# The norms of a delta-rule recurrence: quadrant products or wide products on TensorE

## What is computed

```python
kk = heads(k * k_k)
kk = kk / jnp.maximum(jnp.sqrt(jnp.sum(kk * kk, axis=-1, keepdims=True)), 1e-12)
...
S = S * w_t + sa * (kk_t * a_t) + v_t * k_t
y_t = S @ r_t
...
var = jnp.mean(jnp.square(y - mean), axis=-1, keepdims=True)
y = (y - mean) * lax.rsqrt(var + RWKV_GN_EPS) * ln_g + ln_b
```

## Time and profile before

| | |
|---|---|
| time, median of 3 runs | 871.68 us (871.65 to 872.04) |
| profiled execution, first to last instruction | 873.2 us |
| instructions in that span | 17369 |
| PE busy | 815.8 us, 93% |
| DVE busy | 460.3 us, 53% |
| ACT busy | 240.4 us, 28% |
| POOL busy | 278.8 us, 32% |

### The profile page before, as it was taken

One profiled execution on the slowest core, in us unless ns is written; L12 is line 12 of the kernel. 1 busy time (PEld: TensorE's weight loads), 2 busy tenths in 40 slices (PEclk: granted clock), 3 DMA queues, 4 the chain that ended last, 5 costly groups with the idle time before them and its releaser, 6 DMA issues. The chain is left out here.

```text
span 873.2 us, 17369 instructions
## 1 busy us (share of the span) xinstructions
PE 815.8 (93%) x7175; PEld 544.7 (62%) x7175; DVE 460.3 (53%) x1154; ACT 240.4 (28%) x581; POOL 278.8 (32%) x267
## 2 busy tenths in 40 slices
PE   8999999999999999799888999999999999999950
PEld 8557544544444355777777455555788888888830
DVE  3750478887830136467664244434645555454534
ACT  6220111112200143455543112221233223232214
POOL 5810000000499501452741100000135565543332
PEclk9999999999999999999999999999999999999995
DMA  9934433445111123000000881112889989888639
GB/s 315 324 90 135 145 120 121 139 158 172 37 38 36 27 70 133 18 3 4 4 4 20 308 325 48 49 73 96 325 296 301 303 285 273 277 267 261 206 73 367
DMA packets 79719, 136.35 MB, mean 156 GB/s; under 512 B 17213, under 2 KB 51226, under 8 KB 79642
## 3 DMA queue, kind: packets, MB, share of 16 engines
q1 hardware_dynamic: 69338, 118.44, 39.0%
q0 software_dynamic: 10304, 16.82, 8.2%
HBM read 124.18 MB, written 29.92 MB: 176 GB/s over the span
## 5 line engine op out<-in xcount | busy, mean ns | idle before, releaser
L792 PE MATMUL banks<-REG_W 128*128 128x512 f32 (+2 forms) x832 | 274.6, 499 | 0.9 <-DVE pend L1988 0.5
L792 PEld LDWEIGHTS banks<-REG_W 128*128 128x128 f32 (+1 forms) x832 | 125.9, 182 | 135.3 <-issue 133.8
L792 PE MATMUL banks<-REG_W,REG_Y 128*128 128x512 f32 x256 | 118.3, 599 | 1.4 <-DVE REG_Y L2236 1.1
L1434 ACT ACTIVATE REG_P<-banks 128x256 f32<-128x256 f32 (+2 forms) x126 | 53.5, 463 | 156.8 <-PE banks L792 137.7
L792 PE MATMUL banks<-REG_P 64*64 64x64 f32 (+3 forms) x2752 | 79.5, 230 | 13.1 <-issue 8.9
L792 PEld LDWEIGHTS banks<-REG_P 64*64 64x64 f32 (+1 forms) x2752 | 67.6, 135 | 23.0 <-issue 16.4
L1434 ACT ACTIVATE REG_Y<-banks,mod,s 128x128 f32<-128x128 f32 x136 | 51.2, 457 | 85.8 <-PE banks L1386 85.8
L792 PEld LDWEIGHTS banks<-REG_W,REG_Y 128*128 128x128 f32 x256 | 45.6, 191 | 44.3 <-issue 44.2
L792 PEld LDWEIGHTS banks<-REG_Y,REG_P 128*128 128x128 f32 (+1 forms) x616 | 63.1, 181 | 7.0 <-issue 7.0
L792 PE MATMUL banks<-REG_Y,REG_P 128*128 128x128 f32 (+1 forms) x616 | 66.6, 276 | 0.1
L636 POOL TENSOR_TENSOR REG_P<-REG_P 128x1040 f32<-128x1040 f32 x2 | 4.8, 2390 | 175.8 <-DVE REG_P L1801 175.8
(11 more groups left out here) (295 smaller groups left out, 1108.1 us busy)
## 6 DMA issues: line engine op xcount, KB each, us to landing
REG_P<-in_w_ada SPq DMA_DIRECT2D x20, 1024.0 KB, 6.2
REG_W<-in_w_in SPq DMA_DIRECT2D x17, 512.0 KB
REG_P<-in_moe_w_gate SPq DMA_DIRECT2D x17, 512.0 KB, 8.3
REG_W<-in_moe_w_gate SPq DMA_DIRECT2D x16, 512.0 KB, 6.4
REG_W<-in_moe_w_up SPq DMA_DIRECT2D x16, 512.0 KB, 10.7
REG_W<-in_moe_w_down SPq DMA_DIRECT2D x16, 512.0 KB, 16.7
REG_P<-in_moe_w_up SPq DMA_DIRECT2D x14, 512.0 KB, 14.9
REG_P<-in_moe_w_down SPq DMA_DIRECT2D x12, 512.0 KB, 21.2
```

The costliest lines, as they stand in the source:

```text
L792: return pe.matmul(o_, l, r, start=start, stop=stop, skip_group_check=True)
L1434: return act.activation(o_, i_, f, **kw)
```

## The change

The six norms inside the turns use the same wide functions as numbers 1 and 8. The sums become 4 products of 128x128 by 2 columns, the turn one transpose to 8 rows of 128, the spreading 4 products with 8 rows of weights and 128 columns. Inside the turns the results lie elsewhere than for the outer two: the sums in columns 256 to 263 of bank 4, the turned roots in bank 6, the spread ones in banks 6 and 7. The semaphores count one for each step in place of two.

```diff
+            def outer(k):
+                return k in (front_norm(0), tail_norm(TURNS - 1))
+
             def norm_sums(k, squares, count):
...
+                at = 0 if outer(k) else 256
                 for n in range(2):
                     for p in range(2):
-                        c = n * 4 + p * 2
+                        c = at + n * 4 + p * 2
                         last = mm(PS[4][:, c:c + 2], squares[:, p, n * P:(n + 1) * P], bones[:, 0:P:64])
                 last.then_inc(s["w_ss"], 1)
 
             def norm_flip(k):
                 pe.wait_ge(s["w_nrp"], k)
-                pe.transpose(PS[4][0:8, P:2 * P], nrp[:, 0:8], ident[:, :]).then_inc(s["w_nrt"], 1)
+                pe.transpose(PS[4 if outer(k) else 6][0:8, P:2 * P], nrp[:, 0:8], ident[:, :]).then_inc(s["w_nrt"], 1)
 
             def norm_back(k):
...
                 for p in range(2):
                     for n in range(2):
-                        last = mm(PS[5][:, p * W2 + n * P:p * W2 + (n + 1) * P], sel[0:8, n * 2 + p, :], nrT[0:8, :])
+                        at = p * W2 + (n * P if outer(k) else 0)
+                        last = mm(PS[5 if outer(k) else 6 + n][:, at:at + P], sel[0:8, n * 2 + p, :], nrT[0:8, :])
                 last.then_inc(s["w_nrb"], 1)
-
-            corners = ((0, 0), (1, 1), (1, 0), (0, 1))
-
-            def turn_sums(k, squares, count):
...
-                        for h, c in corners:
-                            last = mm(PS[4 + h][cr(c), at:at + 1], squares[hb(h), p, n * P + CH * c:n * P + CH * c + CH],
-                                      ones[hb(h), 0:1])
...
-            def turn_flip(k):
-                pe.wait_ge(s["w_nrp"], k)
-                for c, g in corners:
-                    last = mm(PS[6 + c][hb(g), P:P + CH], nrp[cr(c), :], identq[cr(c), :])
...
-            def turn_back(k):
...
-                for p in range(2):
-                    for n, h in corners:
-                        last = mm(PS[6 + n][hb(h), p * W2:p * W2 + P], sel[cr(n), n * 2 + p, 64 * h:64 * h + 64], nrT[cr(n), :])
...
                         if tail:
-                            turn_sums(tail_norm(m - 1), sqt, tail_squares(m - 1))
+                            norm_sums(tail_norm(m - 1), sqt, tail_squares(m - 1))
...
-                dve.wait_ge(s["w_ss"], 2 * k - 1)
-                ts(nrm[:, :].rearrange("p (a h) -> p h a", h=2), banks[:, 4:6, 256:260], a, b, op0, op1).then_inc(s["w_nrm"], 1)
+                dve.wait_ge(s["w_ss"], k)
+                at = 0 if outer(k) else 256
+                ts(nrm[:, :], PS[4][:, at:at + 8], a, b, op0, op1).then_inc(s["w_nrm"], 1)
...
-                dve.tensor_copy(nrT[:, :].rearrange("p (c t) -> p c t", c=2), banks[:, 6:8, P:P + CH]).then_inc(s["w_nrT"], 1)
+                dve.wait_ge(s["w_nrt"], k)
+                dve.tensor_copy(nrT[0:8, :], PS[4 if outer(k) else 6][0:8, P:2 * P]).then_inc(s["w_nrT"], 1)
```

More of the change, by code:

```diff
@@ L1179, in turn @@
                         pe.wait_ge(s["w_tha"], min(m + 2, TURNS))
-                        turn_flip(tail_norm(m - 1))
+                        norm_flip(tail_norm(m - 1))
                     if tail and l == 4:
-                        turn_back(tail_norm(m - 1))
+                        norm_back(tail_norm(m - 1))
                     if more and l == 4:
-                        turn_sums(front_norm(m + 1), sq, front_squares(m + 1))
+                        norm_sums(front_norm(m + 1), sq, front_squares(m + 1))
                     for n in range(2):
@@ L1204, in turn @@
                         pe.wait_ge(s["w_nbu"], tail_norm(m - 1))
-                    turn_flip(front_norm(m + 1))
+                    norm_flip(front_norm(m + 1))
                 for p in range(2):
@@ L1222, in turn @@
                 if more:
-                    turn_back(front_norm(m + 1))
+                    norm_back(front_norm(m + 1))
                 for n in range(2):
@@ L1529, in squash @@
                     act.wait_ge(s["w_lora"], m)
-                    act.wait_ge(s["w_ss"], 2 * front_norm(m - 1) - 1)
+                    act.wait_ge(s["w_ss"], front_norm(m - 1))
                 z6 = pT[:, B_LORA, PAD + m * W2:PAD + (m + 1) * W2]
@@ L1931, in norm_turned @@
             def norm_turned(k):
[L1932 to L1936, removed]
-                dve.tensor_copy(nrT[:, :].rearrange("p (c t) -> p c t", c=2), banks[:, 6:8, P:P + CH]).then_inc(s["w_nrT"], 1)
+                dve.wait_ge(s["w_nrt"], k)
+                dve.tensor_copy(nrT[0:8, :], PS[4 if outer(k) else 6][0:8, P:2 * P]).then_inc(s["w_nrT"], 1)
             def back(k):
-                if k in (front_norm(0), tail_norm(TURNS - 1)):
-                    dve.wait_ge(s["w_nrb"], 1 if k == front_norm(0) else 2 * k - 2)
+                dve.wait_ge(s["w_nrb"], k)
+                if outer(k):
                     return PS[5].rearrange("p (a n t) -> p a n t", a=2, n=2)
-                dve.wait_ge(s["w_nrb"], 2 * k - 1)
                 return banks[:, 6:8, :].rearrange("p n (a x) -> p a n x", a=2)[:, :, :, 0:P]
```

13 lines of the change are left out of this document (removed).

## The result

The changed kernel takes **873.58 us** (median of 16 runs, 871.08 to 877.47), the kernel before, run beside it, 871.66 us (16 runs). The ratio is 1.0026, 95% interval 1.0015 to 1.0037: slower by 2.3 us, between 1.3 and 3.2. The forecast was 875.4 us in a range of 871.0 to 881.0, slower by 0.2 to 1%.

The account below looks back on a forecast made before the run. PE was taken as the bound, held at times by instruction packets about 3.85 us apart. Added PE time 12.3, less 2.9 hidden, less 5.7 from fewer packets, gave +3.7 us: 875.4 us, range 871.0 to 881.0.

Parts of the forecast that it names:

- What bounds the turns: In the recurrence's four turns, PE is the bound and at times stands until its next instruction packet arrives, 9.9 us.
- The 3.85 us of the prediction: In dense stretches of the turns, two instruction packets of PE in a row cannot start closer than about 3.85 us.
- Time on PE, +12.3 us: Wide sums, turn and spreading of six norms, at 0.11 us a load plus switches, lengthen PE's work by 12.3 us.
- I take 0.2 us each way: Around each wide set on PE, going from quadrants to the whole array and back costs 0.2 us each way.
- What is hidden, -2.9 us: In four places of the turns PE waits anyway for ACT or DVE, which covers 2.9 us of the added work.
- The other three covers: DVE waits after the tail's sums, 0.5 us, after the front's spreading, 1.1 us, and before turn 3, 0.7 us.
- What fewer packets give back, -5.7 us: 468 fewer PE records in the turns are 1.86 packets, 7.1 us; four fifths of it, 5.7 us, comes back.
- The walk through a turn: In turn 0 both later pauses go; in turns 1 to 3 boundaries partly only move, hence four fifths of 7.1.
- The four turns longer by about 4 us: Sign expected in the profile after: the recurrence's four turns last about 4 us longer, mostly the turns with two norms.
- The feed gives nothing back: Rival: in the turns packet boundaries only move and dense packets pause as before; +9.4 us, 881.1 us; chance 0.15.
- The feed decides, faster: Rival: wide work fits under 3.85 us a packet in the turns; -7.1 us, 864.6 us, or half, 868.1; chance 0.10.
- No difference: Rival: with array switches at half, 0.1 us each way, the change nets +0.1 us, 871.8 us, not measurable; chance 0.20.

Follow-up runs that it names:

- 64 columns: The change with the wide sums of the six inner norms moving 64 columns in place of 2, against the kernel before: 873.75 us, ratio 1.0013.
- change again: The changed kernel run once more, unaltered, against the kernel before: 874.86 us, ratio 1.0029.
- change, sums twice: The change with the wide sums of the six inner norms computed twice, against the kernel before: 882.62 us, ratio 1.0100.
- quadrant sums twice: The kernel before with the quadrant sums of the six norms computed twice, 384 records more, nothing wide: 877.87 us, ratio 1.0068.
- bfloat16 squares: The kernel before with squares and ones of the norms' sums in bfloat16, 192 records fewer inside the turns: 869.46 us, ratio 0.9970.
- the three parts: Wide forms put into the kernel before for the six inner norms: sums alone, ratio 1.0006; spreading alone, 1.0010; turn and spreading, 1.0007.

## Why the prediction was right, and where its sum was off

**What bounds the turns: right.** PE is the bound and packets of its program hold it. Both directions with nothing made wide moved the time as the step said, +5.9 us for 384 records more and -2.6 for 192 fewer, though the profile of the second shows no gain in the turns. The packets of the instruction queue are in the trace themselves: of the 29 distances from one start to the next in the four turns of the kernel before, 22 lie between 3.4 and 4.2 us, and in none of the twelve profiles is one under 3.28 us. The 3.85 us of the prediction are thus a middle value and not the least distance. The Trainium skill, "Runtime: NRT & Kernel Launch", section "Instruction fetch mechanics", lets the crossing from block to block be mostly hidden; in these dense stretches the runs disagree.

**Time on PE, +12.3 us: too high.** With the change and 64 columns the clock stayed at full, so it shows this term by itself. The four turns of the kernel before, then of that one:

```profile
340.30:478.10 137.80, 120.13 (x3821) 103.76 (x3821) 87.77 (x185) 69.41 (x185) 58.00 (x42) 1.00 0.08 27
```

```profile
338.70:476.00 137.30, 127.40 (x3587) 109.48 (x3586) 87.59 (x185) 69.37 (x185) 58.00 (x42) 1.00 0.08 27
```

PE is busy 7.3 us longer, in turns that are no longer: 5.0 us less than the 12.3. The pace of 0.11 us was right. The step that failed is "I take 0.2 us each way" for every set: leaving took 0.99 - 0.88 = 0.11 us behind the sums and 0.21 - 0.11 = 0.10 behind the turn, 0.21 only behind the spreading, and in turns 1 and 2 the spreading passes directly into the front's sums, so one way in is not paid. From the rows of turn 1, without any way in: 6 x (0.99 + 1.09 + 0.21) = 13.7 us, less 6 x (0.46 + 0.44 + 0.13) = 6.2 for the quadrants, is 7.5 us, close to the 7.3. With 13 ways in that would be paid (sums 4, turn 3, spreading 6), at 0.2 us, it makes 10.1 us, an estimate; the busy time does not show these 2.6 us. The prediction's upper bound of 14.7 us is a slip: 5.0 us and 36 switches of 0.3 us are 15.8.

**What is hidden, -2.9 us: seen in part.** The tail's turn waits for ScalarE for 0.50 us as before, so its way in is free. The other three covers (2.3 us) have no run of their own. By the two rows above PE's idle time in the turns fell from 17.67 to 9.90 us, by 7.8 us; 6.7 of these are pauses without a releaser, so the other waits shrank by 1.1 us.

**What fewer packets give back, -5.7 us: too low.** The pauses fell by 7.0 us (9.9 to 2.9), with 64 columns by 6.7 (to 3.2). The walk through a turn kept a fifth back for boundaries that only move; nearly all of what could go went.

**The sum.** With the estimate for the ways in it is 10.1 - 2.3 - 6.7 = +1.1 us in place of 3.7. That meets the +1.1 us of the change at full clock (64 columns; 0.1 to 2.2) and the change's own runs above 0.98 (872.41 - 871.66 = +0.75 us), but it is no proof, for the terms that the profiles measure give 7.3 - 1.1 - 6.7 = -0.5 us. So at full clock the terms nearly cancel, and where the remaining microsecond is lost is not shown. Two single executions can't show it: in all runs the time is 1.7 to 1.9 us above the profiled span, so the profile of the kernel before (873.2 us) belongs to an execution of about 875 us, 3 us above the median, while that of 64 columns (872.16 us) lies 1.6 us below its own.

**What the prediction lacked: the clock.** It names the granted clock nowhere. The medians leave 1.2 to 1.4 us of the measured 2.3 to 2.5 to the runs in which the clock falls to half; the overlap of the intervals keeps this an estimate. What a fall costs is read from turn 2, here with the other turns, from the first weight load of each (us, one execution each):

| | turn 0 | turn 1 | turn 2 | turn 3 | together |
|---|---|---|---|---|---|
| before | 36.19 | 34.30 | 33.49 | 33.84 | 137.82 |
| after | 36.23 | 34.89 | 35.18 | 32.67 | 138.97 |
| change again | 35.72 | 34.68 | 34.80 | 32.89 | 138.09 |
| 64 columns | 35.68 | 35.22 | 33.69 | 32.72 | 137.31 |
| change, sums twice | 37.07 | 39.25 | 35.66 | 33.18 | 145.16 |
| quadrant sums twice | 37.90 | 35.99 | 34.65 | 33.11 | 141.65 |
| bfloat16 squares | 35.77 | 34.79 | 34.59 | 33.30 | 138.45 |

Turn 2 has a fall in the second and third row: 1.5 and 1.1 us more than with 64 columns. "The four turns longer by about 4 us" was thus wrong: 1.2 us with two falls, not longer at all without. That the first turn would be nearly unchanged holds; that turns 1 and 2 carry the most holds too, while turn 3, with one norm, even became shorter by 1.2 us. That forecast and result agree in size is in part luck: one term was too high where another was missing.

**The rivals.** "The feed gives nothing back" fell by the pauses, by the three parts and by the doubled quadrant sums; with fewer records its value is the very edge of the interval. "The feed decides, faster" fell too: it wanted 3.6 to 7.1 us less, and the change is slower, with 64 columns as well. "No difference" came near for the work itself: at full clock the parts are within it.

## What to carry to other kernels

In a dense stretch of small PE products count the instruction records as well as the PE time: here one record more or less was worth some 15 ns with its work, and work put in place of records fills the pauses first (PE 7.3 us busier, 6.7 us fewer pauses) and lengthens the stretch once they are gone. Before replacing small products by wide ones with few columns, look at the granted clock by stretches and at its mean in several executions; a median can hold two kinds of runs that one profile doesn't show. When a forecast comes out near, test its terms all the same.

## What the hardware showed that was not expected

The granted clock fell to half inside a stretch in which PE's records leave no gap: 2.00 us busy of 2.00 in 427 to 429 us of the kernel after, and half clock from 429.7. What PE did there was wide products of two columns behind wide products of eight rows. With 64 columns in the first kind, the mean clock was low in none of 11 runs, against 10 of 12 beside them, and the one profile has no fall in the turns. The Trainium skill, "TensorE: Matmul & The Clock Gate", Part 1, lets the clock follow how busy PE has been; busy time as the profile counts it did not show this fall coming.
